# Tile 1's last three heads, its merging, output products and residual, moved behind tile 0's norm and among the first expert rows

## The reference

```
z     = h @ w_in + b_in                          # q, k, v of 8 heads of 64, two gates
p     = softmax([q k^T / 8 + bias, q k_ctx^T / 8])   # 256 own keys, 256 keys of the context
y_na  = (p @ [v; v_ctx]) @ w_na_out
mix   = (gate_hy * y_hy + gate_na * y_na) @ w_out
x     = x + g1 * mix
h     = rmsnorm(x) * g * (1 + sc2) + sh2
q     = h @ peer_w_q                              # 8 heads, two halves of 128
s     = q . peer_keys                             # 128 keys for each half
idx,g = the 16 best of the 16 x 16 sums, softmax over them
out   = sum_k g_k * gelu(h . u[idx_k]) * v[idx_k] # 16384 experts, 8 heads x 16 per token
x     = x + g2 * out
```

## Time and profile before

| | |
|---|---|
| median of 3 runs | 2466.39 us |
| the profiled execution | 2465.73 us |
| its span, first to last instruction | 2463.9 us |
| TensorE's granted clock, mean | 0.986 |
| busy, share of the span | PE 93%, DVE 65%, ACT 40%, POOL 31% |
| mean busy share of the DMA engines from 1760 us to 1780 us | 0.00 |
| first gather of an expert row issued | 1800.29 us |
| last matmul's start in the chain | 2454.79 us |

### The profile page before, as it was taken

How to read it: one execution, slowest core, us unless ns; L and a number is a source line. 1 busy time by engine, 2 the same in 40 slices (tenths; PEclk the granted TensorE clock), 3 DMA queues, 4 the chain that set the end, 5 groups by cost and what they waited for, 6 DMA issues and landing times.

```text
span 2463.9 us, 31350 instructions
## 1 busy us (share of the span) xinstructions
PE 2295.5 (93%) x11750; PEld 1620.6 (66%) x11750; DVE 1612.2 (65%) x2638; ACT 995.6 (40%) x1628; POOL 756.4 (31%) x618
## 2 busy tenths in 40 slices
PE   6999999999999999999999989999898998877777
PEld 5789999788777677767776567677774554322222
DVE  6868995776555665655755135547578877777764
ACT  2334443434445544444544132013435544444443
POOL 0000000002655665655665400100033443333331
PEclk9999999998999999999999989999899999999999
DMA  9655867465999999999999973036399999999997
GB/s 381 248 210 221 332 270 280 187 239 194 415 420 420 408 410 419 392 421 421 385 420 421 420 303 137 35 117 259 155 354 421 415 421 421 421 422 421 420 421 314
DMA packets 108847, 824.72 MB, mean 335 GB/s; under 512 B 11904, under 2 KB 14336, under 8 KB 15504
## 3 DMA queue, kind: packets, MB, share of 16 engines
q0 software_dynamic: 83520, 608.21, 59.9%
q1 hardware_dynamic: 24448, 212.19, 22.0%
q10 hardware_dynamic: 720, 2.25, 0.3%
HBM read 821.55 MB, written 1.05 MB: 334 GB/s over the span
## 4 chain that ended last, share of the span: by engine, by line
PE 71%; DMA 15%; DVE 8%; issue 3%; ACT 2%; POOL 0%; SPq 0%; DVEq 0%; ACTq 0%; POOLq 0%
DMA ring<-in_uv,arena 11%; PE ps L811 9%; PE ps L813 9%; PE ps L812 9%; PE ps L797 8%; PE ps L1219 7%; PE ps L894 6%; PE ps L1736 5%; PE ps L830 4%; PE ps L1253 4%; DMA arena<-in_uv,arena 3%; PE ps L805 2%; DVE accb L2497 1%; PE ps L1628 1%; PE ps L1065 1%
## 5 line engine op out<-in xcount | busy, mean ns | idle before, releaser
L2521 ACT ACTIVATE arena_r<-ring 128x2048 fp32r<-128x2048 f32 x184 | 352.8, 1917 | 22.7 <-DMA ring<-in_ffn_w_down 13.9
L2085 DVE TENSOR_TENSOR ring_r<-ring,arena_r 128x2048 fp32r<-128x2048 f32 x142 | 325.5, 2292 | 55.7 <-ACT arena_r L2521 52.2
L2521 ACT ACTIVATE arena<-arena 128x1 f32<-128x1 f32 (+6 forms) x617 | 187.9, 305 | 388.7 <-DVE arena L2497 290.5
L1736 PE MATMUL ps<-arena,sel 128*128 128x512 f32 x540 | 256.7, 606 | 48.2 <-ACT sel L2521 47.6
L2521 ACT ACTIVATE arena<-ps 128x256 f32<-128x256 f32 (+1 forms) x228 | 105.7, 464 | 444.1 <-PE ps L805 148.9
L1736 PE MATMUL ps<-ring,sel 128*128 128x512 f32 x484 | 231.4, 607 | 53.2 <-ACT sel L2521 52.9
L3062 POOL DMA_INDIRECT arena<-in_uv,arena x135 | 126.5, 937 | 436.4 <-DVE arena L2352 252.5
L811 PE MATMUL ps<-arena_r 128*128 128x512 f32 (+1 forms) x672 | 242.3, 361 | 0.4 <-DVE arena_r L2085 0.3
L812 PE MATMUL ps<-arena_r 128*128 128x256 f32 (+1 forms) x768 | 228.6, 298 | 0.0
L1736 PEld LDWEIGHTS ps<-arena,sel 128*128 128x128 f32 x540 | 95.3, 189 | 192.0 <-ACT sel L2521 110.8
L2497 DVE CUSTOM_DVE_ANT_0 accb<-arena,ps 128x1024 f32<-128x1024 f32 x135 | 164.8, 1221 | 63.0 <-DMA arena<-in_uv,arena 59.0
(11 more groups left out here) (327 smaller groups left out, 4459.0 us busy)
## 6 DMA issues: line engine op xcount, KB each, us to landing
ring<-in_ada_w SPq DMA_DIRECT2D x24, 1024.0 KB, 9.9
ring<-in_ada_w SPq DMA_DIRECT2D x12, 2048.0 KB, 8.1
ring<-in_w_in SPq DMA_DIRECT2D x10, 2048.0 KB, 12.2
ring<-in_w_ada SPq DMA_DIRECT2D x8, 2048.0 KB, 8.0
ring<-in_ffn_w_gate SPq DMA_DIRECT2D x14, 1024.0 KB, 5.7
ring<-in_ffn_w_up SPq DMA_DIRECT2D x14, 1024.0 KB, 7.0
ring<-in_ffn_w_down SPq DMA_DIRECT2D x14, 1024.0 KB, 7.1
ring<-in_w_out SPq DMA_DIRECT2D x6, 2048.0 KB, 11.2
```

The source lines that it names most:

```text
L1736: last = e.matmul(ps.banks[2 * t + c], m.diag[:, i % NDIAG, :], rows[:, 1024 + 512 * c:1536 + 512 * c], start=(i % 128 == 0), stop=(i % 12 ...
L2085: v(e.tensor_tensor(ring_low[ring.half[unit]], ring.buf[unit], mo.high[unit_at[unit] % NHIGH].bitcast(F32), ALU.subtract), ("low", unit))
L2521: A.mark(e.activation(out, src, func, **kw), name)
```

## The change

It reorders each engine's program; no arithmetic is added or taken away, and no transfer.

- PE: turns 0 to 12 stay. `peer_spread(0)` moves from turn 13 into turn 12, the whole first query comes ahead of turn 13, and turns 14 and 15 go behind `key_scores(0)`, with `tokens(0)` and the second query between them. All of `na(1)` goes behind `key_scores(1)`. `out2(1)` goes into the row loop, one half ahead of row 2's products and one ahead of row 4's.
- DVE: tile 0's norm comes ahead of the softmax work of turns 14 and 15; `scaled(15)` goes into the first head's choices, behind the first index and where `merged_na(1, *)` was; `merged_na(1, *)` goes behind the dot products of rows 1 and 2, `added(1, *)` behind those of rows 5 and 7.
- ACT: the root comes ahead of turn 12's copy, `peer_shift(0)` ahead of `weights(14)`; turns 13 to 15 and `weights(15)` are between the first queries' copies; tile 1's squares move to rows 6 and 8.
- Turns 14 and 15 use banks 6 and 7 in place of 4 and 5. The memory (`m` to `se2`) stays the same.

```diff
-            for i, (h, t) in enumerate(its):
-                b = bank(("turn", i), (4,))
+            def turn(i):
+                b = bank(("turn", i), (4,) if i < 14 else (6,))
...
-                b = bank(("attended", i // 2), (5,)) if i % 2 == 0 else ps.bank["attended", i // 2]
+                b = bank(("attended", i // 2), (5,) if i < 14 else (7,)) if i % 2 == 0 else ps.bank["attended", i // 2]
...
+            for i in range(11):
+                between = first if i < 8 else na0 if i == 8 else out0
+                turn(i)
+                some(between, 1 if i < 8 else 2)
+                attended(i)
+                some(between, 1 if i < 8 else 2)
+            turn(11)
+            attended(11)
+            peer_sums(0)
+            turn(12)
+            peer_spread(0)
+            attended(12)
+            query(0, 0)
+            query(0, 1)
+            turn(13)
+            attended(13)
...
-            some(na1, 1)
             key_scores(0)
+            turn(14)
             tokens(0)
-            some(na1, 4)
-            for n in range(2):
-                query(1, n)
+            attended(14)
+            query(1, 0)
+            turn(15)
+            query(1, 1)
+            attended(15)
             key_scores(1)
-            some(out1, 8)
+            some(na1, 5)
             for i in range(256):
+                if i in (2, 4):
+                    some(out1, 4)
...
-            for i in range(16):
-                if i + 2 < 16:
-                    peak(i + 2)
...
+            for i in range(12):
+                peak(i + 2)
...
+                scaled(i + 1)
...
-                if i == 12:
-                    rstd(("norm_peer", 0), pr.scr[:, 2048:2049])
-                if i == 13:
-                    normed(0, range(8))
+            rstd(("norm_peer", 0), pr.scr[:, 2048:2049])
+            normed(0, range(8))
+            peak(14)
+            scaled(13)
+            peak(15)
+            scaled(14)
...
                     yield from experts_of(t, h, 0, 8, 8)
-                    for n in range(2):
-                        merged_na(1, n)
+                    scaled(15)
...
                 if i in (1, 2):
-                    added(1, i - 1)
+                    merged_na(1, i - 1)
+                if i in (5, 7):
+                    added(1, i // 2 - 2)
...
+            for i in range(12):
+                weights(i + 1)
+                turned(i)
+                context_score(i + 2)
...
+            root(("norm_peer", 0), ps.bank["norm_peer", 0][:, 0:1], D, pr.scr[:, 2048:2049])
+            turned(12)
+            weights(13)
+            context_score(14)
+            peer_shift(0, range(8))
+            weights(14)
+            context_score(15)
...
             query(0)
+            turned(13)
+            attended(13)
+            weights(15)
             key_scores(0)
+            turned(14)
+            turned(15)
             query(1)
+            attended(15)
             key_scores(1)
...
-                if i in (2, 3):
-                    peer_squares(1, i - 2)
+                if i in (6, 8):
+                    peer_squares(1, i // 2 - 3)
```

More of the change, by code:

```diff
@@ L1540, in scores @@
                     at.append((bank(("score", j), SCORES), r, h // 2, t))
-                for c, k in ((0, m.kn), (256, m.kc)):
+                for c, k in ((0, se2.kn), (256, se2.kc)):
                     for j, (b, r, p, t) in enumerate(at):
-                        last = e.matmul(b[:, c:c + 256], m.qn[r, p, 128 * t:128 * t + 128], k[r, p, :],
+                        last = e.matmul(b[:, c:c + 256], se2.qn[r, p, 128 * t:128 * t + 128], k[r, p, :],
                                         start=True, stop=True)
@@ L1635, in pe @@
             some(first, 1)
-            for i, (h, t) in enumerate(its):
-                b = bank(("turn", i), (4,))
+            def turn(i):
+                b = bank(("turn", i), (4,) if i < 14 else (6,))
                 e.wait_ge(*V["scaled", i])
-                P.mark(turned(b, [m.pt[i % 2][:, 128 * k:128 * k + 128] for k in range(4)]), ("turn", i))
+                P.mark(turned(b, [se2.pt[i % 2][:, 128 * k:128 * k + 128] for k in range(4)]), ("turn", i))
                 if i % 2 and i + 3 < len(its):
@@ L1641, in pe, with attended @@
                     scores(i + 3)
[L1642 to L1651, removed]
-                b = bank(("attended", i // 2), (5,)) if i % 2 == 0 else ps.bank["attended", i // 2]
+            def attended(i):
+                h, t = its[i]
+                b = bank(("attended", i // 2), (5,) if i < 14 else (7,)) if i % 2 == 0 else ps.bank["attended", i // 2]
@@ L1653, in pe @@
                 e.wait_ge(*A["turn", i])
                 r = slice(64 * (h % 2), 64 * (h % 2) + 64)
[L1655 to L1666, removed]
+                P.mark(summed(b[r, 0:128], [(se2.vs[k][:, 64 * h:64 * h + 64],
+                                             se2.pt[i % 2][:, 128 * k:128 * k + 128]) for k in range(4)]),
+                       ("attended", i))
@@ L2333, in peak @@
                 emptied(("score", i))
-                v(e.tensor_reduce(m.st[:, 4 * (i % 2):4 * (i % 2) + 1], s, AX.X, ALU.max, negate=True), ("peak", i))
+                v(e.tensor_reduce(se2.st[:, 4 * (i % 2):4 * (i % 2) + 1], s, AX.X, ALU.max, negate=True), ("peak", i))
             def scaled(i):
-                p_, c3 = m.pt[i % 2], 4 * (i % 2)
+                p_, c3 = se2.pt[i % 2], 4 * (i % 2)
                 e.wait_ge(*A["weights", i])
-                v(e.reciprocal(m.st[:, c3 + 2:c3 + 3], m.st[:, c3 + 1:c3 + 2]))
-                v(e.tensor_scalar(p_, p_, m.st[:, c3 + 2:c3 + 3], None, ALU.mult), ("scaled", i))
+                v(e.reciprocal(se2.st[:, c3 + 2:c3 + 3], se2.st[:, c3 + 1:c3 + 2]))
+                v(e.tensor_scalar(p_, p_, se2.st[:, c3 + 2:c3 + 3], None, ALU.mult), ("scaled", i))
             def merged_hy(i):
@@ L2377, in dve @@
             peak(1)
-            for i in range(16):
-                if i + 2 < 16:
-                    peak(i + 2)
[L2381 to L2384, removed]
+            for i in range(12):
+                peak(i + 2)
+                if i == 5:
+                    ring.emptied["bias", 0] = V.now
+                scaled(i + 1)
                 if i < 4:
@@ L2876, in context_score @@
             def context_score(i):
-                a(m.sc[i % 2][:, 256:512], taken(("score", i))[:, 256:512], ACT.Copy, ("context score", i), scale=0.125)
+                a(se2.sc[i % 2][:, 256:512], taken(("score", i))[:, 256:512], ACT.Copy, ("context score", i), scale=0.125)
             def weights(i):
@@ L2883, in weights @@
                     e.wait_ge(*P["attended", i - 2])
-                a(m.pt[i % 2], m.sc[i % 2], ACT.Exp, ("weights", i), bias=m.st[:, c3:c3 + 1],
-                  accum_out=m.st[:, c3 + 1:c3 + 2])
+                a(se2.pt[i % 2], se2.sc[i % 2], ACT.Exp, ("weights", i), bias=se2.st[:, c3:c3 + 1],
+                  accum_out=se2.st[:, c3 + 1:c3 + 2])
             context_score(0)
@@ L2900, in peer_shift, with turned, attended @@
                     a(hT[:, k, c], hT[:, k, c], ACT.Identity, ("hT peer", t, k), bias=mod[2][:, 24 + k:25 + k])
[L2901 to L2904, removed]
+            def turned(i):
+                a(se2.pt[i % 2], taken(("turn", i)), ACT.Copy, ("turn", i))
                 emptied(("turn", i))
-                if i + 2 < 16:
-                    context_score(i + 2)
+            def attended(i):
+                e.wait_ge(*P["attended", i])
+                c, t = i // 2 % 4, i // 8
+                a(se2.yna[:, c, 128 * t:128 * t + 128], ps.bank["attended", i // 2][:, 0:128], ACT.Identity,
+                  ("attended", i), bias=pvc("b_in", 20 + c))
+                emptied(("attended", i // 2))
+            for i in range(12):
+                weights(i + 1)
+                turned(i)
+                context_score(i + 2)
                 if 4 <= i < 8:
```

2 lines of the change are left out of this document (1 added, 1 removed).

## The result

The changed kernel has a median of 2482.4 us (2479.74 to 2484.69, 4 runs) against 2466.5 for the kernel before on the same chips: ratio 1.0064, 95% interval 1.0052 to 1.0077. That is 15.9 us more; 2478.5 had been forecast, with a range of 2471 to 2486. The profiled execution's span is 2480.7 us, 16.8 more than before.

A forecast was written before the change was run, and what follows sets the result against it. The prediction took full DMA transfers from 1836 us at 420 GB/s as the bound, set by bytes delivered before. A 5.2 MB debt costs 12.4 us: 2478.1 from the profiled execution, 2478.8 from the median; forecast 2478.5, range 2471 to 2486.

The forecast's parts named there:

- The gate at row 7: Row 7's gather waits for tile 1's second half of output products: out at 1834.6 us in place of 1820.65.
- first index: Tile 0's norm and first query come earlier, so the first gather goes out at 1795.4 us, 4.8 us earlier.
- the rest of `mix2(1, 0)`: First half of tile 1's output products: the remaining 7/8 take 6.3 us behind the gated sum, to 1821.6.
- the sum's delay: VectorE's gated sum, needed by tile 1's output products, is ready at 1815.2 us in place of 1802.5.
- the conversion of row 7's delay into time: At row 7's data start, 11.5 MB delivered against 16.7; the missing 5.2 MB at 0.42 MB/us cost 12.4 us.
- The break-even point: Row 7's issue at 1821 us gives no change; it must be by 1816 for the full gain.
- a sign of being wrong: The end moving by another amount than the bytes missing at 1836 us over 0.42 would show the forecast wrong.
- The cross-check: DMA engines start 5 us earlier, idle about 4 us ahead of rows 5 and 6 and 7.5 ahead of row 7.
- the faster rival: Only the first index's 4.8 us earlier start counts, with buffers free in time: 2461.6 us; chance 0.07.
- The case of no change: Waits of both halves of the output products are hidden: about 2466 us, within 0.2%; chance 0.05.
- The one of a second hold-up behind row 7: With 10 buffers and a late start, row products hold up gathers again behind row 7: 2484 to 2492 us; chance 0.06.
- TensorE as the pace: TensorE's work alone sets the end, finishing its run-up 5.3 us later: 2471.7 us; chance 0.08.

The follow-up runs named there:

- products ahead: Changed kernel with both halves of tile 1's output products ahead of the row loop, merging left behind rows 1 and 2: 2478.02 us, ratio 1.0049.
- second half late: Changed kernel with the second half of tile 1's output products ahead of row 6 in place of row 4: 2486.14 us, ratio 1.0080.
- kept busy: Changed kernel with 8 extra matmuls of 256 columns on TensorE ahead of the first half of tile 1's output products: 2479.37 us, ratio 1.0056.
- interleaved alone: Kernel before the change with only the halves of tile 1's output products moved ahead of rows 2 and 4, additions and squares following: 2483.57 us, ratio 1.0066.
- merging alone ahead: Changed kernel with both merged_na steps ahead of row 0's dot products, output products still ahead of rows 2 and 4: 2481.23 us, ratio 1.0051.
- both ahead: Changed kernel with both merged_na steps ahead of row 0's dot products and both halves of the output products ahead of the row loop: 2469.42 us, ratio 1.0014.
- turn 15 ahead: Changed kernel with turn 15 before the second query, scaled(15) before the first choices, merging inside them, output products before the row loop: 2467.36 us, ratio 0.9998.
- the same, early load: The turn 15 ahead kernel with 1.57 MB of the last query weights loaded right after the last scores: 2464.24 us, ratio 0.9990.
- before, early load: Kernel before the change with 1.57 MB of the last query weights loaded right after the last scores: 2465.33 us, ratio 0.9995.

## Why the prediction was right, and which terms were too small

All kernels together, from their traces (span less the issue of row 7's gather):

| kernel | row 7 out | span | difference |
|---|---|---|---|
| before | 1820.65 | 2463.9 | 643.3 |
| changed | 1838.02 | 2480.7 | 642.7 |
| products ahead | 1832.62 | 2475.4 | 642.8 |
| second half late | 1840.62 | 2483.7 | 643.1 |
| kept busy | 1833.49 | 2476.4 | 642.9 |
| interleaved alone | 1837.30 | 2480.2 | 642.9 |
| merging alone ahead | 1837.16 | 2480.1 | 642.9 |
| both ahead | 1822.94 | 2466.8 | 643.9 |
| turn 15 ahead | 1823.24 | 2468.2 | 645.0 |
| the same, early load | 1819.47 | 2462.6 | 643.1 |
| before, early load | 1819.67 | 2462.6 | 642.9 |

**What held.** The gate at row 7 sets the end; in nine of eleven traces the span is 642.7 to 643.3 us behind it, over 21 us of shift. In the other two, both parts ahead and turn 15 ahead, the bytes due before row 7 are not through in time, and it is up to 2 us more. The path to it was right step by step: first index 1795.14 (1795.4), row 3 1807.19 (near 1808), row 4 1816.31 (near 1816). The transfers stay full behind row 7. The gain in the first index is real, 5.2 us, and is wasted.

**The first term too small** is the rest of `mix2(1, 0)`, 6.3 us in the prediction. It took 9.29, for the clock was low. The prediction weighed the low clock for the first query only and gave the output products the full clock of the earlier trace rows, from a kernel where they had no gap ahead of them. The change itself makes the gap. This is 3.0 of the 3.4 us by which row 7 came later than forecast; most of the rest is the sum's delay of 0.6, for which row 2's data were late. The rule of the Trainium skill that the prediction named (TensorE: Matmul & The Clock Gate, "Part 1: The HAM clock gate") was applied to the wrong stretch. Where it says that the cost varies from run to run, the traces agree: 9.29 us in one, 6.52 in another with the same order.

**The second** is the conversion of row 7's delay into time. The prediction had row 7 14.0 us later and charged 12.4. It let row 7's data flow at the full rate from 1.2 us behind the issue, and compared with the bytes that the old kernel had at 1836. But the rate comes up only by 3 us behind the issue (the last section): from 1839 to 1843 the new kernel moves 1.15 MB, where the full rate would give 1.68, and that is 1.3 us. The old kernel had delivered all it might by 1822 (11.5 MB, as the earlier trace rows give it), stood behind the same gate, and had paid for a like start by 1836 (1.12 MB from 1821 to 1825). So the delay counts nearly in full: the measured one of 17.4 gave 16.8, and one of 14.0 would have been some 14 us by the table. The break-even point that the prediction worked out (an issue at 1821 gives no change) said this already; the sum didn't use it. The prediction named as a sign of being wrong an end that moves by another amount than the bytes missing at 1836, and that is what came: they were 5.1 MB, 12.3 us, and the span grew by 16.8. The count of bytes is right once both kernels are at the full rate: 16.7 us at 1844. The early load in the kernel before, where the transfers are through by row 7, shows that a byte moved out of the stretch ahead of the gate gives nothing there: if each counted, it should have given 3.7 us, by the gate nothing, and it gave 0.8, with an interval from 3.5 less to 1.0 more and 20.3 us from first gather to row 7 as ever.

**A wrong reading beside the sum.** The cross-check says that the DMA engines start 5 us earlier, and the faster rival that no transfer runs ahead of the index. The first line here is of the kernel before, the second of the changed one:

```profile
1792.00:1794.00 2.00, 2.00 (x20) 2.00 (x20) 0.00 (x0) 0.15 (x2) 0.00 (x0) 1.00 1.02 426
1790.00:1796.00 6.00, 3.81 (x31) 3.47 (x32) 5.24 (x27) 0.04 (x1) 0.86 (x1) 1.00 0.00 0
```

Before the change the SyncE loads fill the engines from 1790 on, up to the first gather; with the change the loads go out at 1798.71 in place of 1789.70, and nothing moves until row 0's data from 1796 on. Only the first gather is earlier; the transfers start 6 us later. The sum didn't use this, and ahead of a late gate at row 7 it costs nothing (the kernel with the interleaving alone has its early loads and pays as much as the whole change); with the gate on time it is what is left (both parts ahead).

**The rivals.** The faster case fell with the changed kernel and, as far as the first gather alone goes, with both parts ahead: 4.7 us of earlier index, 3.8 us slower. No kernel here has an earlier index with all loads and products where they were, so what the index would be worth then stays open. The case of no change is excluded by the interval. The one of a second hold-up behind row 7 isn't seen: there the gathers go out 1.24 us apart and the engines stay full. TensorE as the pace fell with the first experiment (TensorE behind with its work, and the span 5.3 us shorter) and with the interleaving alone (2474 at most by it, 2483.57 measured).

**Open.** What decides whether the clock falls in the gap of 3 us ahead of the first half, and whether extra matmuls prevent it, wasn't settled: one execution without them kept the clock. It was low in the kernel with the products ahead too (16.41 us for 120 instructions, against 13.66 with both parts ahead). It fell to 0.50 also behind TensorE's pauses in the kernels with the interleaved products alone (9.05 us) and with the merging alone ahead (4.45 us), but came back to 1.00 during the products of rows 0 and 1 there (5.86 and 5.44 us for 8 instructions, 3.60 at the full clock), so the output products had it.

## What to carry to other kernels

When a long stretch is bound by transfers that go out in order, find the last issue in its run-up that is held by something other than the transfers, and put every delay there in full on the end, as long as the transfers ahead of it are through by then; work that is moved "between the first rows" is moved ahead of that issue or behind it, and only this matters. An earlier first gather is worth nothing while a later one in the same queue waits longer; and look at when the engines start to move anything, since other queues feed them too. Of two steps that block in a row, moving one alone gives little: here 3.5 us and at most 2.4 us each alone, 12.1 together.

## Not expected of the hardware

A gather that goes out into idle engines takes long to be of use: row 7's was issued at 1838.02, and VectorE's dot products on it began at 1843.65, 5.6 us later, where in the full stretch one arrives every 2.5 us. Row 5's, which also found the engines idle (issued at 1825.66), took the same 5.6. Neither is alone: the next gather follows 1.24 us behind it and shares the engines.

```profile
1831.25 1.22 DVE L2503 CUSTOM_DVE_ANT_0 accb<-ring,ps 128x1024 f32<-128x1024 f32 x1 [4.18 <-DMA ring<-in_uv,arena]
...
1843.65 1.22 DVE L2503 CUSTOM_DVE_ANT_0 accb<-ring,ps 128x1024 f32<-128x1024 f32 x1 [6.36 <-DMA ring<-in_uv,arena]
```

In the first microseconds behind the issue little moves:

```profile
1838.00:1839.00 1.00, 1.00 (x11) 1.00 (x10) 0.00 (x0) 0.00 (x0) 0.94 (x1) 1.00 0.00 0
1839.00:1840.00 1.00, 1.00 (x6) 0.52 (x5) 0.00 (x0) 0.58 (x2) 0.74 (x1) 1.00 0.66 98
1840.00:1841.00 1.00, 1.00 (x4) 0.38 (x3) 0.00 (x0) 0.90 (x4) 0.69 (x2) 1.00 0.63 205
1841.00:1842.00 1.00, 1.00 (x4) 0.49 (x3) 0.00 (x0) 0.92 (x3) 0.69 (x2) 1.00 0.93 393
```

It takes until 1841, 3 us behind the issue, for the transfers to come near their full rate. The kernel before pays much the same behind its row 7 (1.12 MB in the four us from 1821, against 1.15 here in those from 1839), which is why it cancels in the difference of their spans.
